# Stick-breaking attention beside the projections: the transposes of the attention weights go ahead of the value products in 24 steps

## The reference: what is computed

```python
for start in range(0, s_, Q_BLOCK):
    z = einsum('bqhd,bkhd->bhqk', q[:, start:end], k[:, :end]) * scale
    log_not = where(strict, log_sigmoid(-z), 0.0)
    tail = cumsum(log_not, axis=3, reverse=True) - log_not
    weights = where(strict, exp(log_sigmoid(z) + tail), 0.0)
    outs.append(einsum('bhqk,bkhd->bqhd', weights, v[:, :end]))
```

## Time and profile before

| | us |
|---|---|
| median of 3 runs | 1277.57 (1276.2 to 1277.68) |
| the profiled execution | 1276.93 |
| its span, first to last instruction | 1275.0 |
| TensorE busy in the span | 1254.1 (98%) |
| VectorE / ScalarE / GpSimd busy | 832.5 / 513.0 / 234.5 |
| steps of the attention | about 42.9 to 339 of the span |

### The profile page before, as it was taken

The page is one execution under the profiler, slowest core; times in us unless marked ns, Lnnn a source line. Parts: engine busy times, 40 slices in busy tenths (PEclk is TensorE's granted clock), DMA queues, the critical chain, the costliest instruction groups (busy, mean ns, idle before and its releaser), DMA issues.

```text
span 1275.0 us, 16443 instructions
## 1 busy us (share of the span) xinstructions
PE 1254.1 (98%) x6120; PEld 1011.2 (79%) x6120; DVE 832.5 (65%) x1002; ACT 513.0 (40%) x794; POOL 234.5 (18%) x157
## 2 busy tenths in 40 slices
PE   7999999999999999999999999999999999999997
PEld 6777777777787888888878888888888888888886
DVE  4546646646397546634787777767686777787863
ACT  5435535547675225213433242424232423233441
POOL 0000000052300002610221111111111121212118
PEclk9999999999999999999999999999999999999999
DMA  6101001110004212110211211111111212111113
GB/s 244 50 34 34 33 33 34 33 50 17 1 1 149 67 67 83 66 34 4 80 67 33 67 50 49 49 49 66 39 60 57 67 39 66 33 67 33 66 58 125
DMA packets 22803, 71.93 MB, mean 56 GB/s; under 512 B 2528, under 2 KB 2784, under 8 KB 22752
## 3 DMA queue, kind: packets, MB, share of 16 engines
q1 hardware_dynamic: 22752, 71.22, 16.4%
HBM read 67.02 MB, written 4.19 MB: 56 GB/s over the span
## 4 chain that ended last, share of the span: by engine, by line
PE 68%; DVE 11%; issue 9%; ACT 5%; DMA 3%; POOL 2%; DVEq 1%; SPq 0%; ACTq 0%; POOLq 0%
PE ps L736 14%; PE ps L738 14%; PE ps L737 14%; PE ps L1095 4%; PE ps L1094 4%; PE ps L1093 4%; DVE w_lo L607 3%; DVE conv_ff L1960 2%; PE ps L831 2%; PE ps L814 2%; ACT conv_ff L1518 2%; DMA down_raw<-u_down 2%; DMA raw<-u_up 1%; PE ps L790 1%; ACT w_hi L602 1%
## 5 line engine op out<-in xcount | busy, mean ns | idle before, releaser
L736 PE MATMUL ps<-x_hi,w_hi 128*128 128x512 f32 x336 | 139.3, 414 | 8.5 <-DVE x_lo L1714 7.3
L1093 PE MATMUL ps<-mix_hi,w_hi 128*128 128x512 f32 x352 | 137.1, 389 | 0.9 <-DVE partial L1991 0.9
L1094 PE MATMUL ps<-mix_lo,w_hi 128*128 128x512 f32 x352 | 136.9, 389 | 0.0
L1095 PE MATMUL ps<-mix_hi,w_lo 128*128 128x512 f32 x352 | 136.9, 389 | 0.0
L738 PE MATMUL ps<-x_hi,w_lo 128*128 128x512 f32 x336 | 132.4, 394 | 0.0
L737 PE MATMUL ps<-x_lo,w_hi 128*128 128x512 f32 x336 | 131.9, 393 | 0.0
L2012 DVE TENSOR_TENSOR acc<-acc,ps 128x512 f32<-128x512 f32 x144 | 95.6, 683 | 42.5 <-PE ps L738 42.2
L2279 POOL TENSOR_TENSOR weight_sums<-raw 128x512 f32<-128x512 f32 x22 | 32.0, 1452 | 471.4 <-DMA raw<-u_up 471.4
L736 PE MATMUL ps<-h_hi,w_hi 128*128 128x512 f32 x288 | 113.7, 395 | 1.5 <-DVE acc L2012 0.6
L737 PE MATMUL ps<-h_lo,w_hi 128*128 128x512 f32 x288 | 112.2, 390 | 0.0
L738 PE MATMUL ps<-h_hi,w_lo 128*128 128x512 f32 x288 | 112.1, 389 | 0.0
(11 more groups left out here) (264 smaller groups left out, 2723.1 us busy)
## 6 DMA issues: line engine op xcount, KB each, us to landing
raw<-u_up SPq DMA_DIRECT2D x44, 512.0 KB, 3.3
raw<-u_in SPq DMA_DIRECT2D x22, 512.0 KB, 3.3
down_raw<-u_down SPq DMA_DIRECT2D x38, 256.0 KB, 2.7
x_stage<-u_x SPq DMA_DIRECT2D x8, 512.0 KB, 8.8
raw<-u_out SPq DMA_DIRECT2D x8, 512.0 KB, 3.3
x_nat<-x_nat SPq DMA_DIRECT2D x8, 512.0 KB, 3.3
raw<-u_gate SPq DMA_DIRECT2D x8, 512.0 KB, 3.2
out<-o_norm SPq DMA_DIRECT2D x7, 512.0 KB, 2.6
```

What stands on the lines that cost most here:

```text
L736: mm(dst, w_hi, x_hi, start=first, stop=False)
L1093: mm(dst, w_h[:, k], t_h[:, kt, :], start=fresh and kt == 0, stop=False, skip_group_check=True)
L1094: mm(dst, w_h[:, k], t_l[:, kt, :], start=False, stop=False, skip_group_check=True)
L1095: last = mm(dst, w_l[:, k], t_h[:, kt, :], start=False, stop=kt == 3, skip_group_check=True)
```

## The change

In TensorE's program the call of `turn_weights` (or `turn_values`) moves ahead of the two calls of `values`. Since bank 6 is now written before the two buffers have been read, ScalarE's copy gets a wait of its own: it may overwrite `un[kb % 2]` only when the value product of two key blocks ago is done.

```diff
@@ -868,13 +868,13 @@
-            if t - 1 in TASK_AT and BANK_TASKS[BANK_AT[t - 1]][4] % 2 == 0:
-                values(BANK_AT[t - 1] - 1)
-                values(BANK_AT[t - 1])
             if t in TASK_AT:
                 turn_weights(BANK_AT[t])
             elif t in BANK_AT:
                 turn_values(BANK_AT[t])
+            if t - 1 in TASK_AT and BANK_TASKS[BANK_AT[t - 1]][4] % 2 == 0:
+                values(BANK_AT[t - 1] - 1)
+                values(BANK_AT[t - 1])
             for pc in (BY_STEP[t] if t < NTICK else []):
                 piece(*pc)
@@ -1322,6 +1322,8 @@
             if n in TASK_AT:
                 _, k, kb = AV_TASKS[TASK_AT[n]]
+                if TASK_AT[n] >= 2:
+                    eng.wait_ge(av_done, TASK_AT[n] - 1)
                 c0 = P if kb == 2 * k + 1 else 0
```

## The result

| us | before | after |
|---|---|---|
| median of 18 runs each | 1276.55 (1275.66 to 1277.73) | 1279.28 (1277.33 to 1280.22) |
| ratio | | 1.0019, 95% interval 1.0013 to 1.0026 |
| span of the profiled execution | 1275.0 | 1278.3 |
| first score matmul to first transpose of the scan stage ("the stretch") | 42.91 to 339.05: 296.14 | 42.14 to 340.76: 298.62 |

The change makes the kernel slower: by 2.7 us between the medians, and by a ratio of 1.0019, right at the 0.2% that the prediction took as the least a measurement can tell. The sum was +2.37 us; the stretch that the change touches is longer by 2.48 us. The median of 1277.57 that the forecast stood on was one of three runs and lay 1.0 us over that of 18, so the absolute forecast, 1279.9, came out 0.6 us high while the difference was 0.4 us low.

The account below looks back on a forecast made before the run. The prediction took TensorE's own queue to bound the attention stretch. Its terms, 0.75 + 0.15 + 1.20 + 0.37 - 0.10 = +2.37 us, on the median 1277.57 gave 1279.9 us, range 1277.0 to 1282.5.

Parts of the forecast that it names:

- switch: On TensorE, a change of array shape between neighbouring matmuls (128*128, 128*64, 64*128), priced at 0.10 us.
- ordinary steps: Attention steps 8, 10, 12, 19, 21 and 27, no scores ahead: two switches either way, +0.05 us each.
- steps 23 and 25: Attention steps with scores ahead: three switches behind the scores instead of two, +0.20 us each, +1.20 over six.
- The unknown price: TensorE's spacing from transposes to value products, taken with a 0.10 us switch; sum between -0.1 and +6.5 us.
- The wait that moved: Step 8, second pair: transposes wait for ScalarE's late copy with value products queued behind; +0.42 us, +0.37 beyond the 0.05.
- The new wait: ScalarE's copy waits for the value product freeing its buffer, starts about 0.4 us sooner; costed at nothing.
- absorbed: Third pair: a transpose's 0.2 us wait on ScalarE swallows the 0.05 of the two steps before it, -0.10 us.
- A free switch: Transposes to value products: the load slips in under short transposes, the order costs nothing; 1277.5 us, chance 0.21.
- the gain through idle time: Attention window: ScalarE's copy, some 0.4 us sooner in 24 steps, takes up TensorE's idle time; 1275.0 us, chance 0.04.
- third rival: Transposes to value products: a switch out of transposes runs the array empty, +6.5 us, 1284.1 us; chance 0.13.
- The low end: Transposes to value products: a free switch, 0.44 instead of 0.54 us, 2.4 us less, a sum of -0.1.
- rival 4: Attention window: faster, as ScalarE's sooner copy takes up TensorE's idle time, ceiling 2.14 us; 1275.0 us, chance 0.04.

Follow-up runs that it names:

- interleaved kernel: Against the changed kernel: in 18 four-transpose steps, each head's two transposes alternate with one key block's value products; stretch 303.68 us, time 1284.43 us, ratio 1.0058.

## Why the prediction was right

**The order that wasn't in the trace.** The prediction built it from pieces: transposes among projection pieces, value products alone, a switch between. That sum held to 0.01 us a step in the ordinary steps and in steps 23 and 25. Even so the 17 ordinary steps came to 0.75 us, 0.10 less than forecast. The unknown price, the spacing from transposes to value products, was taken as 0.54 and measured 0.53; behind scores it was taken as 0.37 for two and 0.59 for four, and measured 0.37 (119.05 to 119.42) and 0.59. The interleaved kernel confirms the price at more places.

**The wait that moved.** The place and the mechanism were right. The size was 0.42 against 0.47 us. The forecast let the transposes start where the value product had started, at 167.32, and they started at 167.40, 0.14 and not 0.05 behind the end of the same copy. The 0.14 could have been read before: in step 11 of the third pair the copy ends at 274.86 + 0.60 = 275.46, the transposes start at 275.60. In return the value products followed 0.56 behind them, not 0.59. The wait shown is 1.03 us; about 0.9 was forecast.

**ScalarE.** The new wait cost TensorE nothing that the list of waits or the spacings show, and the copy of step 10 comes 0.51 us sooner (0.4 forecast). That won nothing: TensorE did not wait for this copy before. The one wait that became shorter, in the third pair, did so as the forecast's "absorbed" term says, 0.10 us: its copy follows GpSimd and not the value products, so what TensorE had lost in the two steps before came off the stop. The interleaved kernel, which lost 0.7 us in the same two steps, took up the whole stop, 0.37 us.

**Rivals.** A free switch is excluded by the spacing and by the interleaved kernel, and the gain through idle time by the list of waits. The prediction mis-sized its third rival. Waiting for the recorded end of the last transpose would put the value products 0.60 us behind the first one, the recorded time of four (80.48 0.60), and not 0.71: the 0.44 already holds the last transpose's own spacing of 0.11, so only 0.27 - 0.11 = 0.16 comes on top, 0.06 over the forecast's 0.10. Its sum is then about 2.37 + 24 x 0.06 = +3.8 us and not +6.5, 1281.4 us, inside the stated range. The measured 0.53 excludes it all the same, but by 0.07 us a place and not by 0.18. The low end, 2.37 - 2.4, is -0.03 and not -0.1. The ceiling of rival 4, all idle time, was too low: a stop can cost more than the idle time shown for it (0.8 against 0.58 us).

**The sum.** +2.37 forecast, +2.48 in the stretch, +2.7 in the medians. The difference of the last two, 0.2 us, is inside the interval of the ratio (1.7 to 3.3 us), and no part of the program behind the stretch is shown to change. That the sum came so close to the stretch is in part luck: the 0.10 us too much for the ordinary steps made up for part of the 0.15 us of drift, which the forecast had no term for, and of the 0.05 too little for the stalled step. The forecast lay on the line between same and slower, and the prediction gave the two nearly even chances.

**The drain.** The rule of the Trainium skill, "TensorEngine Tiling (Array Packing)", Key Properties, that a change of tiling mode drains TensorE, pointed the right way: where one such change more stood in a step, it lost 0.20 us instead of 0.05. The runs give about 0.1 us for the change itself and about 0.15 with the late start behind it. A drain up to the recorded end is not what the rows show: in all 24 places of the changed kernel the value products start 0.06 to 0.08 us ahead of the recorded end of the transposes, where inside a piece a matmul starts 0.16 ahead of the recorded end of the one before it. That end is modelled, so whether the array was empty can't be read from it.

**What isn't shown.** That a change of the array's shape is what costs is read from the rows: transposes and pieces are different work of one shape, and between them nothing is lost; where the shape changes, 0.10 us or a little more is. No run changed the shape and left the rest of an instruction as it was.

## What to carry to other kernels

Where TensorE is the bound, giving another engine its input sooner is worth nothing unless TensorE waits for that engine; read the list of waits first. Its idle time is not quite the ceiling: add for each stop the overlap that it costs, here 0.22 us at one stop and 0.16 at another. When instructions of different array shapes are reordered, count the changes of shape between neighbours in each step: here a step with one change more lost as much as four steps without. And when an instruction that needs fresh data is put ahead of one that doesn't, the one behind stops filling the wait.

## What the runs showed that I had not expected

A stop costs more than its idle time: 0.58 us idle in the middle of the value products, 0.8 us gone when the wait was taken away; and 0.21 us idle ahead of a transpose that started 0.37 us late (0.60 against 0.23 behind the last piece matmul). The rest is hidden in the recorded end of the matmul ahead, which would otherwise have been overlapped. And an effect of 0.1% can be read in the timeline to a few hundredths of a us when TensorE is almost never idle: the stretch came out at 298.62 and 298.63, and at 296.14 twice, while whole runs of one kernel spread over 2 us or more.
